# A hand-ordered two-layer encoder on one core: five places in the instruction order of its mixer are rearranged

## The reference

```
for l in range(2):
    x = layer_norm(ALPHA*x + 0.5*swiglu(x, gate[l,0], up[l,0], down[l,0]))
    x = layer_norm(ALPHA*x + hybrid_mix(x))          # the part that is changed
    x = layer_norm(ALPHA*x + cross_attention(x, mem))
    x = layer_norm(ALPHA*x + 0.5*swiglu(x, gate[l,1], up[l,1], down[l,1]))

hybrid_mix: proj = x @ w_in, cut into three groups of heads
  differential attention, 4 heads of two maps each: a = softmax(q0 k0) - lam * softmax(q1 k1); out = a @ v
  mLSTM, 4 heads: (q k^T * decay) v over max(|den|, exp(-m)), then a norm and a gate
  S5: a complex diagonal recurrence per channel group, GELU, a gated product
  out = concat(A: columns 0-511, B: 512-767, C: 768-1023) @ w_out
cross_attention: q = x @ wq; k, v = mem @ wkv; softmax(q k^T) v @ wo   (mem does not depend on x)
```

## Time and profile before

| what | value |
|---|---|
| median of 3 runs | 1278.38 us (1278.25, 1278.38, 1279.62) |
| the profiled execution | 1279.68 us |
| its span, first to last instruction | 1277.9 us |
| PE busy | 1247.8 us, 98% |
| DVE busy | 775.6 us, 61% |
| ACT busy | 597.5 us, 47% |
| POOL busy | 160.7 us, 13% |
| mean granted clock of TensorE | 0.996 |

### The profile page before, as it was taken

How to read it: one execution, slowest core, us unless ns; L and a number is a source line. 1 busy time by engine, 2 the same in 40 slices (tenths; PEclk the granted TensorE clock), 3 DMA queues, 4 the chain that set the end, 5 groups by cost and what they waited for, 6 DMA issues and landing times.

```text
span 1277.9 us, 16246 instructions
## 1 busy us (share of the span) xinstructions
PE 1247.8 (98%) x6768; PEld 1068.6 (84%) x6768; DVE 775.6 (61%) x1019; ACT 597.5 (47%) x699; POOL 160.7 (13%) x161
## 2 busy tenths in 40 slices
PE   7999999999999999999999999999999999999997
PEld 6888888888889888888888888889888898788886
DVE  5667746686655565445467676566757756654554
ACT  5444554547444554443444435545456444544341
POOL 1036800000101000000000068200001100000000
PEclk9999999999999999999999999999999999999999
DMA  9755555532356276555666555545324535655650
GB/s 333 255 185 178 188 174 165 165 100 87 113 197 211 99 232 197 187 179 194 198 198 198 186 179 196 174 157 176 104 84 130 182 116 165 197 188 177 195 197 34
DMA packets 160233, 219.45 MB, mean 172 GB/s; under 512 B 6912, under 2 KB 136064, under 8 KB 160160
## 3 DMA queue, kind: packets, MB, share of 16 engines
q1 hardware_dynamic: 156864, 206.60, 49.7%
q0 software_dynamic: 3152, 11.76, 2.9%
q10 hardware_dynamic: 144, 0.07, 0.0%
HBM read 217.34 MB, written 1.05 MB: 171 GB/s over the span
## 4 chain that ended last, share of the span: by engine, by line
PE 87%; DVE 6%; ACT 3%; DMA 2%; issue 1%; SPq 1%; POOL 0%; DVEq 0%; POOLq 0%; ACTq 0%
PE PS L519 26%; PE PS L521 25%; PE PS L520 25%; DVE WL L1602 2%; PE PS L550 2%; ACT WH L1186 1%; PE PS L602 1%; PE PS L1105 1%; PE PS L1129 1%; DMA RAW<-in_ffn_w_down 1%; SPq L408 1%; PE PS L808 1%; DVE X L1641 1%; PE PS L885 1%; PE PS L841 1%
## 5 line engine op out<-in xcount | busy, mean ns | idle before, releaser
L1602 DVE TENSOR_TENSOR WL<-RAW,WH 128x2048 fp32r<-128x2048 f32 (+1 forms) x199 | 448.1, 2256 | 258.6 <-ACT WH L1186 258.2
L1186 ACT ACTIVATE WH<-RAW 128x2048 fp32r<-128x2048 f32 (+1 forms) x199 | 370.7, 1871 | 160.5 <-DMA RAW<-in_ffn_w_up 119.3
L519 PE MATMUL PS<-WH,XH 128*128 128x512 f32 x768 | 306.9, 400 | 4.7 <-DVE WL L1602 2.6
L521 PE MATMUL PS<-WH,XL 128*128 128x512 f32 x768 | 300.4, 391 | 0.0
L520 PE MATMUL PS<-WL,XH 128*128 128x512 f32 x768 | 300.1, 391 | 0.0
L519 PEld LDWEIGHTS PS<-WH,XH 128*128 128x128 f32 x768 | 144.7, 188 | 36.3 <-issue 3.8
L521 PEld LDWEIGHTS PS<-WH,XL 128*128 128x128 f32 x768 | 144.6, 188 | 30.7
L520 PEld LDWEIGHTS PS<-WL,XH 128*128 128x128 f32 x768 | 144.9, 189 | 28.5 <-issue 0.5
L519 PE MATMUL PS<-WH,HH 128*128 128x512 f32 x352 | 137.6, 391 | 0.1
L521 PE MATMUL PS<-WH,HL 128*128 128x512 f32 x352 | 137.1, 389 | 0.0
L520 PE MATMUL PS<-WL,HH 128*128 128x512 f32 x352 | 137.0, 389 | 0.0
(11 more groups left out here) (339 smaller groups left out, 1789.6 us busy)
## 6 DMA issues: line engine op xcount, KB each, us to landing
RAW<-in_ffn_w_down SPq DMA_DIRECT2D x88, 512.0 KB, 4.4
RAW<-in_ffn_w_gate SPq DMA_DIRECT2D x87, 512.0 KB, 4.0
RAW<-in_ffn_w_up SPq DMA_DIRECT2D x87, 512.0 KB, 5.0
RAW<-in_w_in SPq DMA_DIRECT2D x44, 512.0 KB, 4.5
RAW<-in_xattn_wkv SPq DMA_DIRECT2D x32, 512.0 KB, 4.1
RAW<-in_xattn_wq SPq DMA_DIRECT2D x16, 512.0 KB, 4.0
RAW<-in_w_out SPq DMA_DIRECT2D x12, 512.0 KB, 4.4
RAW<-in_xattn_wo SPq DMA_DIRECT2D x12, 512.0 KB, 4.0
```

The source lines that it names most:

```text
L519: nc.tensor.matmul(out_ap, sh, mh, start=first, stop=False)
L521: return nc.tensor.matmul(out_ap, sl, mh, start=False, stop=last)
L1186: return nc.scalar.activation(dst, src, ACT.Copy)
L1602: return v.tensor_tensor(dst, full, hi.bitcast(F32), ALU.subtract)
```

## The change

Five pieces of the order change; no instruction is added or removed, on any engine.

1. DVE: `diff_max(l, 0)` moves from behind `s5_states(l, 1)` to ahead of it.
2. ACT: `diff_exp(l, 3)` moves ahead of a `split()`; in layer 1 that `split()` moves further, behind `cat_high(l, 0)`.
3. PE: `mlstm_scores(l, 0)` moves ahead of unit K3 in layer 0, and the wait for all four decays stands behind it (in layer 1, which has no K3, that wait goes and each `mlstm_scores` has only its own).
4. PE: the transposes of the last two heads move inside a unit: between the two halves of V1 in layer 0, of W3 in layer 1. ACT's `cat_high(l, 2)` and DVE's `cat_low(l, 2)` follow, one `split()` (unit V2) going ahead of each.
5. DVE: in `boundary(l, 1)` the `split()` of V3 moves behind the first half's `norm_scale`. Small exchanges in DVE's `mix`: in layer 0 one `split()` goes behind `mlstm_sums`, in layer 1 one behind `mlstm_scale`, and `diff_sums(l, 2)` goes ahead of `diff_stats(l, 0)`.

```diff
@@ -696,7 +696,7 @@
                     mm = nc.tensor.transpose(PS[:, 7, i * P:i * P + P], MEMX[:, t, c * P:c * P + P], ident)
                 mm.then_inc(mem_psum.sem, 1)

-            def memory_unit(key, b):
+            def memory_unit(key, b, between=None):

                 u = UNIT[key]
                 if key[1] == "K":
@@ -710,6 +710,8 @@
                     for c in range(KC):
                         mm = prod(PS[:, b, t * 256:t * 256 + 256], MH[:, c, tok], ML[:, c, tok],
                                   wh[:, c, :], wl[:, c, :], c == 0, c == KC - 1)
+                    if t == 0 and between is not None:
+                        between()
                 mm.then_inc(unit_used.sem, 1)

             def fill_around(where, l, nl, nn):
@@ -1038,9 +1040,10 @@
                 spread(l)
                 diff_out(l, 1)
                 diff_turn(l, 2)
-                pe.wait_ge(decay_done.sem, decay_done.at(l, HEADS))
-                mid(l, 1, 3)
                 mlstm_scores(l, 0)
+                if FILL["mid", l]:
+                    pe.wait_ge(decay_done.sem, decay_done.at(l, HEADS))
+                    mid(l, 1, 3)
                 mlstm_scores(l, 1)
                 diff_out(l, 2)
                 diff_scores(l, 3)
@@ -1069,12 +1072,20 @@
                 pe.wait_ge(b_ready.sem, b_ready.at(l, 1))
                 turn_cat(l, CATM, 0, 5)
                 rows_product(w + 2, [0, 1], CH, CL, False, False)
+                def last_heads():
+                    pe.wait_ge(a_ready.sem, a_ready.at(l, 2))
+                    turn_cat(l, CATA, 2, 7)
+
                 pe.wait_ge(cat_lo.sem, cat_lo.at(l, 2))
-                rows_product(w + 3, [4, 5], CH, CL, False, False)
-                fill_read("mid", l, 2)
-                mid(l, 3, 4)
-                pe.wait_ge(a_ready.sem, a_ready.at(l, 2))
-                turn_cat(l, CATA, 2, 7)
+                if FILL["mid", l]:
+                    rows_product(w + 3, [4, 5], CH, CL, False, False)
+                    fill_read("mid", l, 2)
+                    memory_unit(FILL["mid", l][3], 4, last_heads)
+                else:
+                    unit_ready(w + 3)
+                    rows_tile(w + 3, [4, 5], CH, CL, 0, False, False)
+                    last_heads()
+                    rows_tile(w + 3, [4, 5], CH, CL, 1, False, False).then_inc(unit_used.sem, 1)
                 w = UNIT[l, "W", 4]
                 unit_ready(w)
                 wh = WH[w % RING][:, :].rearrange("p (c n) -> p c n", c=2)
@@ -1500,20 +1511,22 @@
                     diff_turned(l, 2)
                 mid_out(l, 1, 3)
                 diff_evac(l, 2)
-                split()
                 diff_exp(l, 3)
+                if FILL["mid", l]:
+                    split()
                 diff_turned(l, 3)
                 cat_high(l, 0, 0, 5)
                 if not FILL["mid", l]:
+                    split()
                     split()
                 mid_out(l, 2, 4)
                 diff_evac(l, 3)
                 mid_split(l, 3)
                 cat_high(l, 1, 4, 5)
                 split()
+                split()
+                cat_high(l, 2, 2, 7)
                 mid_out(l, 3, 4)
-                cat_high(l, 2, 2, 7)
-                split()
                 split()
                 split()

@@ -1716,8 +1729,6 @@
                 if n == 3 and l + 1 == DEPTH:
                     end(l, last)
                     return
-                if n == 1:
-                    split()
                 if n == 2:
                     norm_scale(l, n, 0)
                     if not FILL["ffn2", l]:
@@ -1725,6 +1736,8 @@
                 norm_sum(l, n, 1, last)
                 if n != 2:
                     norm_scale(l, n, 0)
+                if n == 1:
+                    split()
                 norm_center(l, n, 1)
                 norm_var(l, n, 1)
                 if n == 1 or n == 2 and FILL["ffn2", l]:
@@ -2043,8 +2056,8 @@
                 split()
                 split()
                 s5_states(l, 0)
+                diff_max(l, 0)
                 s5_states(l, 1)
-                diff_max(l, 0)
                 gates_in(l)
                 split()
                 conv(l, 0)
@@ -2085,16 +2098,16 @@
                     decay_scores(l, 2)
                     decay_scores(l, 3)
                     diff_max(l, 3)
+                    mlstm_sums(l)
                     split()
-                    mlstm_sums(l)
                     mlstm_scale(l)
                     cat_low(l, 0, 0, 5)
                     diff_sums(l, 3)
                 else:
                     decay_scores(l, 0)
                     decay_scores(l, 1)
+                    diff_sums(l, 2)
                     diff_stats(l, 0)
-                    diff_sums(l, 2)
                     diff_combine(l, 2)
                     decay_scores(l, 2)
                     decay_scores(l, 3)
@@ -2104,8 +2117,8 @@
                     mlstm_sums(l)
                     cat_low(l, 0, 0, 5)
                     diff_sums(l, 3)
+                    mlstm_scale(l)
                     split()
-                    mlstm_scale(l)
                     split()
                     cat_low(l, 1, 4, 5)
                 diff_combine(l, 3)
```

## The result

| | median | lowest to highest | runs |
|---|---|---|---|
| before | 1278.35 us | 1278.25 to 1279.62 | 4 |
| changed kernel | 1269.61 us | 1269.44 to 1269.85 | 4 |

The ratio is 0.993 with a 95% interval of 0.9917 to 0.9943: 8.7 us faster. The prediction was 1270.8 us, 1.2 us too high and inside its range, 0.6 us above the range's low end. The changed kernel's profiled execution took 1269.51 us.

The account below looks back on a forecast made before the run. PE, busy 98%, bounds the kernel, so only its idle time can be won. Terms sum to 8.18 us: 1271.5 against the profiled execution, 1270.2 against the median; the middle, 1270.8 us, is forecast, range 1269.0 to 1274.2.

Parts of the forecast that it names:

- head 0's maxima: PE's stall at the transposes of head 0 goes in both layers, 1.88 us in layer 0, together 3.76 us.
- scores of head 0: mLSTM scores of head 0 fill PE's stall at the wait for all decays: 0.65 us in layer 0, 0.19 in layer 1.
- exponentials of head 3: Layer 0: run ahead of ACT's split, they remove PE's stall at head 3's transposes; 0.99 us, bounds 0.5 to 0.99.
- last heads: W4's wait for ACT's rounding goes in both layers, with transposes half a unit earlier; 2.09 us, bounds 0 to 2.09.
- splits around the join: PE's transposes of the new x come 0.25 us earlier in each layer; 0.5 us, bounds -0.5 to 0.5.
- The bound of nothing at the next link: Lower bound 0 for head 0's gain: next link just as late; nearest is head 1's transposes, layer 0, 0.05 us slack.
- The clock: Layer 1, 976 to 978 us, granted clock 0.50: the price of the slow stretch was estimated at 1.0 us.
- the join: Rival: the join gives nothing, ACT's copy or V3's split late again; 5.6 us won, about 1273.4; chance 0.10.
- head 0's gain: Rival: it comes back at head 1's chain with 0.05 us to spare; 4.4 won, 1274.6 or between; chance 0.11.
- the loads: Rival: the stream of loads bounds, waits move without shortening the chain; 1278.4 to 1279.6 us; chance 0.05.
- slower: Rival: V2's load lands 10 us late or more, blocking ACT's copy for W4 and PE; 1281 or more; chance 0.02.
- The rival that the slow stretch goes: Half of the clock rival: stretch goes, 1269.8 us, or a second one comes, 1271.8, gains unchanged; chance 0.10 for both.

Follow-up runs that it names:

- e11_before_third: The kernel before, unchanged, profiled a third time; 1278.39 us, one run.
- e1_max0_only: The kernel before with only part 1, head 0's maxima ahead of the second half of the recurrence; 1274.99 us against 1278.74.
- e6_pad_head1: The changed kernel with one more reduction on DVE, result unused, directly ahead of head 1's maxima in layer 0; 1270.82 us.
- e4_last_heads_no_splits: The kernel before with part 4's transposes moved and their ACT copy ahead of V1's evacuation, all splits left in place; 1277.86 us, ratio 0.999.
- e9_before_again: The kernel before, unchanged, profiled once more; 1279.83 us, one run.
- e7_after_again: The changed kernel, unchanged, measured again for comparison; 1270.38 us against 1278.53 for the kernel before.
- e5: The changed kernel with two more reductions on DVE, results unused, ahead of head 0's maxima in layer 0; 1270.89 us.
- e8: The changed kernel with mLSTM scores of heads 2 and 3, in layer 1 also their weighting and copy AT, moved ahead of other work; 1269.14 us.
- e3: The kernel before with part 4 and part 5's moved split in `boundary`; 1275.95 us, ratio 0.9978.
- e2: The kernel before with parts 2 and 3 alone; 1276.98 us, ratio 0.9986.

## Why the prediction held

`e11_before_third` and the changed kernel's profile are a clean pair, since neither has the slow stretch. The differences of PE's starts in the two traces, from one mark to the next (steps under 0.1 us are added to the term ahead of them):

| term | predicted | measured |
|---|---|---|
| head 0's maxima, layer 0 and 1 | 1.88 + 1.88 | 1.95 + 1.94 |
| scores of head 0, layer 0 and 1 | 0.65 + 0.19 | 0.69 + 0.09 |
| exponentials of head 3 | 0.99 | 0.94 |
| last heads, layer 0 and 1 | 1.07 + 1.02 | 0.97 + 0.89 |
| splits around the join | 0.25 + 0.25 | 0.42 + 0.42 |
| sum | 8.18 | 8.31 |
| ahead of the first swap of layer 0 | none | 0.27 |
| the last `turn_x` of layer 1 | none | 0.32 |

8.31 + 0.27 + 0.32 = 8.90 us, and the two profiled executions are 1278.39 - 1269.51 = 8.88 us apart.

**Head 0: right.** The whole delay went in both layers, and `e1_max0_only` shows it alone. The bound of nothing at the next link did not come true, for the reason given: head 1's chain starts from a swap on PE. `e6_pad_head1` shows that its slack was really that small.

**Scores of head 0: right in layer 0, half in layer 1.** ACT's copy released head 2's output as forecast, 0.19 us earlier. But the output now starts behind a stall, and its second matmul comes 0.22 us after the first (959.85, 960.07), where it was 0.12 before (967.22, 967.34 in `e11_before_third`). So 0.10 us was lost at once. `mlstm_num`, which waits for DVE, takes nothing more: the difference of the two profiles is the same on both sides of it.

**Head 3: right**, 0.3 us to spare. The forecast added 0.16 us to this stall where its own rule says 0.15.

**Last heads: right, the size 0.1 us high.** Part of the rest stands one line lower: behind a stall the second matmul of W4 came 0.31 us after the first (371.13, 371.44), in the changed kernel 0.23 (366.31, 366.54), and that 0.08 us is counted at the join.

**Splits around the join: mis-sized twice.** The term was 0.25 us by the step to `turn_x`; measured 0.42, of which 0.26 is that step (0.38 to 0.12), 0.08 W4's restart, and 0.05 the shorter transposes (0.85 to 0.80 us from their start to the next matmul). And the two terms are not independent: `e4_last_heads_no_splits` shows that in layer 0 the term of the last heads depends on this one. The forecast added the two as if each stood alone.

**The baseline: this is where the 1.2 us lie.** The forecast could not say which of 1279.68 and 1278.38 to subtract from, and took the middle, 0.65 us too high. The profiled execution had met the slow stretch, 1.12 us, which is nearly all of the 1.30 it lay above the median. Had the stretch been tied to the profiled execution, the sum would have gone against the median: 1278.38 - 8.18 = 1270.2. The remaining 0.6 us are about the two rows of the table that no edit explains. More than half of each is one wait: at the first swap PE waits 0.39 us for XE in `e11_before_third` and 0.23 in the changed kernel's profile, behind a split of ACT that waits for a load; at the last `turn_x` 0.90 and 0.60 us for DVE's X. At PE's first swap of layer 0 the profiles differ by 0.75 us (0.34 later in `e9_before_again`, 0.41 earlier in the changed kernel's) with the same instructions ahead of it. The changed kernel's own two profiles differ by 0.6 us behind the mixer of layer 1: from there to the last `turn_x` one gains 0.18 us on the profile of before, the other loses 0.38. In the comparison of `e7_after_again` the medians are 1278.53 - 1270.38 = 8.15 us apart, with none of this excess over the sum.

**The clock: the size near, the working wrong.** The 1.0 us was worked out from one window of 2 us. The stretch is longer, 1.7 us of clock were withheld, and a wait hid a third of it, which left 1.12 us. That 1.0 came near is luck.

The rivals: the join gave 2.7 us, where the forecast had 2.59; head 0's gain did not come back; the loads did not bound. The rival "slower" needed V2 to land 10 us late by its text (its own terms give 10.7), and V2 was early. The rival that the slow stretch goes named 1269.8 us, nearer to the measured 1269.61 than the forecast. That is no point for it: the stretch did go from the profile, but most runs behind the median of before had not held it.

## What to carry to other kernels

With the bound engine 98% busy, its own list of waits was the map: every term that came true stood in it. For each wait ask what the awaited engine did ahead of the awaited work, and what that was needed for. Sum the delays, not the idle shown: each stall cost 0.1 to 0.2 us more than its idle time.

An edit that takes a stall away at one place and an edit that clears the next engine's queue belong in one sum. Test them apart before crediting either.

Where a profiled execution is off the median by about a microsecond, look for a stretch at another granted clock before choosing the baseline, in the profile itself and not in the mean clock. And count waits that the change does not touch as noise: here two of them moved one program by 1 us between two profiles.

## What was unexpected of the hardware

The half clock (0.50, 1.2 GHz) came in two of three profiles of the very same program, and in another program once in layer 0 and once in layer 1, each time where PE worked through short products with stalls between them, around head 3. It cost 1.12 us in layer 1 and 1.67 us in layer 0. At the half clock matmuls with 256 columns start 0.21 us apart, at the full clock 0.12 us (`e1_max0_only`, across the return of the clock):

```profile
340.46 0.41 PE L521 MATMUL PS<-WH,ML 128*128 128x256 f32 x1
340.67 0.41 PE L519 MATMUL PS<-WH,MH 128*128 128x256 f32 x1
...
341.22 0.28 PE L519 MATMUL PS<-WH,MH 128*128 128x256 f32 x1
341.34 0.28 PE L520 MATMUL PS<-WL,MH 128*128 128x256 f32 x1
```

At 1.2 GHz 256 columns take 0.213 us, so at the half clock the spacing is one column per cycle. At 2.4 GHz that would be 0.107 us, so 0.01 us of the 0.12 does not follow the clock; no run shows what it is.

Nor is it settled why the changed kernel meets the stretch less. Of 24 runs of it and of `e5`, `e6`, `e7` and `e8` one has a mean clock of 0.997 (the 1272.14 us of `e5_pad_head0`), of before 10 of 37. Of `e1`, `e3` and `e4`, which keep the stalls before head 0's mLSTM scores and at head 3, 8 of 27 runs have 0.996 or 0.997; of `e2`, which takes them away, 1 of 11. That points to these stalls, but the mean is a rough sign, and no run varied the stalls alone to test it.
